# Latent attention: products with the value in groups of four key blocks, with a ring of ten blocks of exponentials

## The reference, cut to what matters

```python
def block(args):
    qn, qr = args
    sc = (jnp.einsum('bqhd,bkhd->bhqk', qn, k_nope)
          + jnp.einsum('bqhr,bkr->bhqk', qr, k_rope))
    p = jax.nn.softmax(sc.astype(jnp.float32) * scale, axis=-1)
    return jnp.einsum('bhqk,bkhd->bqhd', p.astype(v.dtype), v)
```

## Time and profile before

| | us |
|---|---|
| median of three runs | 4700.68 (4699.26 to 4701.24) |
| the profiled execution | 4708.83 |
| its span | 4707.0 |
| TensorE busy | 3914.3 (83%) |
| GpSimd busy | 2345.3 (50%) |
| VectorE busy | 2249.9 (48%) |
| ScalarE busy | 1668.9 (35%) |
| L911, products | 375.0 in 1536 records, 610 ns each |
| L898, rest | 141.6 in 768 |
| L883, scores | 264.4 and 245.7 in 768 each; idle before them 1.8, released by L983 |
| L859, sweeps | 324.8 in 768 |
| L983, exponentials | 372.1 in 384, 1021 ns each; idle before them 735.2, all released by L898 |
| L926, a total, four records | 1.03 at 1023.44 and wherever the clock is full |
| L1006, GpSimd's additions | 804.1 in 336, 2393 ns each |

### The profile page before, as it was taken

The page is one execution under the profiler, slowest core; times in us unless marked ns, Lnnn a source line. Parts: engine busy times, 40 slices in busy tenths (PEclk is TensorE's granted clock), DMA queues, the critical chain, the costliest instruction groups (busy, mean ns, idle before and its releaser), DMA issues. The chain is left out here.

```text
span 4707.0 us, 50767 instructions
## 1 busy us (share of the span) xinstructions
PE 3914.3 (83%) x18860; PEld 2692.3 (57%) x18860; DVE 2249.9 (48%) x3530; ACT 1668.9 (35%) x2737; POOL 2345.3 (50%) x1107
## 2 busy tenths in 40 slices
PE   3999956899996999766969999569999779996778
PEld 1788844455543566444858887345555356654467
DVE  4100004555545999664630001245555279995645
ACT  1001012233334888663110110113333268885610
POOL 0122211477775999801622221117777679994035
PEclk9999968799997999998979999569999889998989
DMA  5212335422304210054432123280322122204153
GB/s 164 78 67 79 118 133 166 101 47 51 87 10 90 47 35 21 13 109 147 168 112 79 68 85 121 107 236 20 87 53 50 32 64 49 49 6 98 32 200 133
DMA packets 138738, 401.30 MB, mean 85 GB/s; under 512 B 15328, under 2 KB 73408, under 8 KB 113728
## 3 DMA queue, kind: packets, MB, share of 16 engines
q1 hardware_dynamic: 138144, 398.46, 29.6%
q10 hardware_dynamic: 384, 0.10, 0.0%
HBM read 247.81 MB, written 150.60 MB: 85 GB/s over the span
## 5 line engine op out<-in xcount | busy, mean ns | idle before, releaser
L1006 POOL TENSOR_TENSOR mla_sum_pool<-mla_sum_pool,mla_probs 128x1024 f32<-128x1024 f32 x336 | 804.1, 2393 | 226.7 <-ACT mla_probs L983 199.7
L1014 DVE TENSOR_REDUCE mla_row_max<-psum 128x1 f32<-128x512 f32 x768 | 522.4, 690 | 506.3 <-PE psum L859 502.2
L1286 DVE TENSOR_REDUCE diff_row_max<-psum 128x1 f32<-128x1024 f32 x512 | 613.0, 1219 | 52.8 <-PE psum L1157 36.2
L1222 ACT ACTIVATE diff_probs<-psum,diff_shift 128x1024 f32<-128x1024 f32 x512 | 566.1, 1111 | 194.6 <-DVE diff_shift L1293 188.8
L983 ACT ACTIVATE mla_probs<-psum 128x1024 f32<-128x1024 f32 x384 | 372.1, 1021 | 735.2 <-PE psum L898 735.2
L328 POOL TENSOR_TENSOR in_w_hi<-in_w_raw,ones 128x1024 fp32r<-128x1024 f32 x44 | 105.3, 2393 | 862.0 <-PE psum L352 763.2
L1151 PE MATMUL psum<-diff_k_op,diff_q_op 128*128 128x512 f32 x1024 | 372.3, 446 | 75.5 <-DMA diff_v_op<-v_d 65.4
L1169 PE MATMUL psum<-ident,diff_probs 128*128 128x128 f32 x2048 | 330.5, 284 | 107.4 <-DVE diff_turned L1320 75.2
L859 PE MATMUL psum<-mla_k_a,mla_q_a 96*128 96x512 f32 x768 | 324.8, 441 | 80.5 <-DVE mla_row_max L1014 40.4
L352 PE MATMUL psum<-in_x_hi,in_w_hi 128*128 128x512 f32 x1408 | 378.6, 391 | 5.7 <-DVE in_x_lo L414 5.7
L1169 PEld LDWEIGHTS psum<-ident,diff_probs 128*128 128x128 f32 x2048 | 216.4, 141 | 285.7 <-issue 193.9
(11 more groups left out here) (179 smaller groups left out, 6297.4 us busy)
## 6 DMA issues: line engine op xcount, KB each, us to landing
raw_d<-in_h_raw SPq DMA_DIRECT2D x28, 1024.0 KB, 4.7
in_w_raw<-in_w_in SPq DMA_DIRECT2D x44, 512.0 KB, 5.5
split_d<-in_h_hi SPq DMA_DIRECT2D x16, 1024.0 KB
split_d<-in_h_lo SPq DMA_DIRECT2D x16, 1024.0 KB
out_o_in<-o_d SPq DMA_DIRECT2D x16, 1024.0 KB, 7.9
out_gate<-raw_d SPq DMA_DIRECT2D x16, 1024.0 KB, 10.0
mla_q_b<-mq_d SPq DMA_DIRECT2D x24, 512.0 KB, 14.9
diff_q_op<-split_d SPq DMA_DIRECT2D x48, 256.0 KB, 8.9
```

The lines of the kernel that those rows point to most:

```text
L1006: nc.gpsimd.tensor_tensor(acc, first, probs[:, s % RING, :], ALU.add).then_inc(pool_added, 1)
L1014: nc.vector.tensor_reduce(row_max[:, u % 2, qb, n:n + 1], psum[:, sweep_bank(g), :], AX.X, ALU.max).then_inc(maxed, 1)
L1222: nc.scalar.activation(dst[:, half * HALF:(half + 1) * HALF].rearrange("p (a n) -> p a n", n=CH), banks(n, m, half), ACT.Exp, bias=shift[: ...
L1286: nc.vector.tensor_reduce(row_max[:, n % 2, m, half:half + 1], banks(n, m, half), AX.XY, ALU.max).then_inc(maxed, 1)
```

## The change

The products are issued four in a row after every second pair of steps (at s = 7, 11, 15, ...), those of the four steps s - 7 to s - 4. Before, two followed every pair, those of s - 3 and s - 2. The ring of exponentials grows from six to ten blocks of 4 KB per partition. ScalarE's copy of a unit's product moves from kb = 2 to kb = 4, and the loops run on for four steps more instead of two.

```diff
-    LEAD, LAG, RING = 4, 2, 6
+    LEAD, GROUP, RING = 4, 4, 10
...
-                    if s % 2:
-
-                        if s < STEPS:
-                            rest(s - 1)
-                            rest(s)
-                        if 3 <= s <= STEPS + 1:
-                            product(s - LAG - 1)
-                            product(s - LAG)
+
+                    if s % 2 and s < STEPS:
+                        rest(s - 1)
+                        rest(s)
+                    if s % GROUP == GROUP - 1 and GROUP <= s < STEPS + GROUP:
+                        for n in range(GROUP):
+                            product(s - 2 * GROUP + 1 + n)
                     if kb == Z_AT and u >= 1:
                         total(u - 1)
...
-                for s in range(STEPS + LAG + 1):
+                for s in range(STEPS + GROUP + 1):
                     u, kb = s // NB, s % NB
-                    if kb == LAG and u >= 1:
+                    if kb == GROUP and u >= 1:
                         raw_out(u - 1)
```

## The result

| | before | changed |
|---|---|---|
| median of 8 runs | 4701.57 us | 4715.87 us |
| ratio, 95% interval | | 1.003, 1.0019 to 1.0041 |
| measured again in another series | 4698.12 | 4713.31, ratio 1.003, 1.0019 to 1.0041 |
| profiled execution, its span | 4708.83, 4707.0 | 4716.57, 4714.8 |
| first rest to the rest of step 178, layer 1 / 2 | 525.84 / 525.49 | 530.34 / 530.51 |

The change makes the kernel 0.3% slower, 14 to 15 us; the interval of the ratio is 9 to 19 us. The forecast was 4709 (+8.4), the range 4694 to 4728. Slower by over 0.2% was the outcome I had given 0.49.

The account below looks back on a forecast made before the run. TensorE's own stream was taken as the bound. Per layer +10.3 us from intervals and division, -6.3 from the clock and +0.2 at the end, times two, gave +8.4 us: 4709 us, range 4694 to 4728.

Parts of the forecast that it names:

- The bound and the releaser: Latent attention: TensorE's own stream is the bound; the 0.81 us before the scores is the products' end, not a wait.
- (a): Intervals that lose both products become 4.62 us like the first one, -0.91 each: 35 of them, -31.9 us per layer.
- (b): Intervals that now have four products cost 1.72 us more each: 43 of them, +74.0 us per layer.
- (c): The total, now in an interval without products, is free: from 6.39 to 4.67 us, ten times, -17.2 us per layer.
- (d): Behind the division the stall costs 0.75 us instead of 2.21, the multiply waiting for GpSimd's addition: -14.6 us per layer.
- (e): Falls of the granted clock behind divisions, 6.4 and 6.1 us in the two layers, disappear: -6.3 us per layer.
- (f): Layer's end, step 178's rest to the last total: +1.15 us, less 0.95 for a total at full clock: +0.2.
- The sum: All terms over both layers: (10.3 - 6.3 + 0.2) x 2 = +8.4 us.
- R1: Slower: half clock stays, falling at the groups' idle stretches as often as behind divisions now: 4722 us; chance 0.14.
- R3: Faster: scores already wait for the second exponential, so intervals without products fall to 3.66 us: 4638 us; chance 0.04.
- R2: The division: without the multiply's wait 4694 us (0.08), with the whole stall kept 4738 us (0.04); chance 0.12.
- R4: Exponentials or products wait for the ring or one another, groups fall apart: unknown sign, some 10 us; chance 0.08.

Follow-up runs that it names:

- the multiply's operand: Changed kernel with the reciprocal left in PSUM, so the multiply reads one operand in SBUF and one in PSUM: 4695.00 us against 4698.12 of before, ratio 0.9992.
- the kernel with the other placing: Changed kernel with its groups of four products at the other pair (s = 5, 9, 13, ...): 4839.58 us against 4696.56 of before, ratio 1.0303.

## Why the prediction was right or wrong

- **The bound and the releaser (right).** I read the 0.81 us of idle weight loading before the scores as the end of the products although the trace names ScalarE. The changed kernel shows the same 0.81 behind four products, with no exponential outstanding ("issue"), and where there are none TensorE is idle for 0.89 us. Halving the exponentials left the first at 0.81 and made the second 0.45. Both were seen in the changed kernel; in the kernel before, the exponentials were not shortened.
- **(a), (b), (c) (right).** Over three traces the intervals are 4.59 to 4.63, 7.23 to 7.27 and 4.65 to 4.68 with a total, against 4.62, 7.25 and 4.67. With the stall taken out by the multiply's operand, the stretch is 521.96 and 521.84; the prediction's parts without the stall are 529.7 - 7.5 = 522.2.
- **(d) the division (mechanism right, 0.1 us short per place).** Multiply over at +9.60 from the rest (forecast +9.55), sweep at +10.25 (+10.2). But the interval is 8.09 to 8.16 where I had 8.00: 0.86 for the stall instead of 0.75, over 20 places +2.2 us. The interval grows by a tenth of a microsecond more than the sweep is late (0.86 for 0.76), and that is the sweep itself, which takes 0.50 after the wait instead of 0.40; the earlier trace rows showed it too (2.21 for 2.11, and a sweep of 0.50). Among the signs I named a multiply near 1.9, the duration before, although my own working (from +7.37 to +9.55) makes it 2.2; it took 2.24.
- **(e) the clock (right in sum, one part by luck).** No half clock in the stretch in any of three traces; behind 0.6 and 0.9 us of idle it never fell. But I put the whole 6.4 and 6.1 us down to falls. In the first layer 0.6 of it was the wait for the third head's load, of which I had said that nothing changes. It went as well, so the sum held. And the first fall of a layer costs 3.1, not 1.5.
- **(f) the end (right within 0.2 per layer).** +1.24 to the last total (forecast +1.15), GpSimd's end at +38.2 as worked out, 0.9 back from the clock.
- **The sum.** For the stage it was +8.4 and the traces give +11.0: 2.2 more from the stall, 0.6 because the kernel before took 0.3 us less per stretch in the mean of six traces than in the one I read, 0.5 outside the stretches, less 0.7 since the other intervals are a hundredth shorter than worked out. The measured 14 to 15 us are 3 to 4 more again. That part isn't explained; the interval of the ratio (9 to 19 us) holds 11 as well as 15, and just misses 8.4.
- **The rivals.** R1 (half clock stays) and R3 (the wait is already there) did not occur. R2's lower end, a multiply of 0.69, is real, but only in an edited kernel, and it gave what was worked out for it (15 forecast and 17 with the right stall, 18 measured). R4: in three traces of the changed kernel all idle time before the exponentials, 710 us, was ended by TensorE's rest and none by the ring. The change of mode that the grouping saves gave nothing, as expected: an interval with four products costs the full 1.72 more, and one without is set by the exponential.
- **What I missed** was the size of the result relative to what can be told: I set 4709 just inside 0.2% and it came out beyond. The direction and the place in the range were forecast; the size was 6 us short. The one term known to be mis-sized is the stall of (d), 0.75 where 0.86 was measured, which is 2.2 us; the larger part, 3 to 4 us, is the unexplained rest.

## What to carry to other kernels

Before regrouping work, ask which idle time its present place covers. Here two products per pair hid the wait for one exponential, with 0.9 us to spare (rest to scores 2.53 where the exponential asks for 1.62). Grouped by four they hid it half of the time, and four steps cost 0.8 us more (4.62 and 7.25 against twice 5.53). Price such a change by intervals between the same two instructions, one kind of interval at a time, and look for the first iteration, where the cover is missing: it gives the price before anything is built. And the repair was elsewhere: VectorE did 5.2 us of work in one piece where 2.7 were free, and given in two pieces, in different steps, the same work cost 51 us less in the two stages.

## What the runs showed of the hardware

- A VectorE multiply of two SBUF operands ended 0.55 us after GpSimd's addition in progress, at every division with sweeps of the kernel before and of the changed one (1.86 and 2.24 us for work of 0.69); with one operand in PSUM it took 0.69 beside the same additions. The Trainium skill (SBUF — State Buffer, "Who interferes with whom") has the rule, and the traces agree.
- TensorE's granted clock after one idle stretch: at 0.6 to 0.9 us it stayed at 2.4 GHz in every interval of three traces; behind the 1.94 us of the kernel before it fell to 1.2 GHz at two or three divisions of ten, the first of the layer always among them; behind 2.85 us at all twenty. A fall cost 3.1 us over two intervals at the first division of a layer and 1.5 at the others in the kernel before; in the kernel with the other placing it made the interval 2.0 us longer and the next one up to 2.4.
